# Thirty token-row dot products of a gated-expert kernel: from one VectorE reduction each to a GpSimd product and a ScalarE accumulating copy

## The reference, cut to what matters

```python
s = jnp.einsum('nhpc,hpkc->nhpk', q, sub_keys)
ts, ti = lax.top_k(s, PEER_TOPK)
...
gate = jax.nn.softmax(best_s, axis=-1)
act = jax.nn.gelu(jnp.einsum('nd,nhkd->nhk', xi, u[idx]), approximate=False)
return jnp.einsum('nhk,nhkd->nd', gate * act, v[idx])
```

## Time and profile before

| what | value |
|---|---|
| median of 3 runs | 2467.96 us (2465.28 to 2469.02) |
| the profiled execution, its own time | 2466.73 us |
| its span | 2465.0 us |
| busy share PE, DVE, ACT, POOL | 95%, 69%, 43%, 25% |
| chain that ended last, by engine | PE 74%, DVE 14%, issue 4%, POOL 3% |
| gate tiles | from 892.59 us to 1089.4 us of the span |
| granted TensorE clock in the gate tiles | 1.00 of full speed (2.4 GHz) |

### The profile page before, as it was taken

How to read it: one execution, slowest core, us unless ns; L and a number is a source line. 1 busy time by engine, 2 the same in 40 slices (tenths; PEclk the granted TensorE clock), 3 DMA queues, 4 the chain that set the end, 5 groups by cost and what they waited for, 6 DMA issues and landing times.

```text
span 2465.0 us, 38176 instructions
## 1 busy us (share of the span) xinstructions
PE 2336.5 (95%) x13568; PEld 1302.4 (53%) x13568; DVE 1707.9 (69%) x2979; ACT 1050.0 (43%) x1496; POOL 612.7 (25%) x494
## 2 busy tenths in 40 slices
PE   7998788999999998989999999988999999999998
PEld 3446664555555566655555555563454444443453
DVE  5326674568899989987888888878353438777235
ACT  4255333565666664543333333344422224333234
POOL 0003361277677651123322222204000010000001
PEclk9998999999999999999999999999999999999999
DMA  5200003378788778889999999923233323332321
GB/s 177 77 26 1 1 1 102 124 263 302 279 302 319 253 226 320 331 305 362 389 361 362 359 362 362 363 95 94 86 112 103 101 77 105 102 102 94 103 85 52
DMA packets 164871, 470.79 MB, mean 191 GB/s; under 512 B 17616, under 2 KB 70736, under 8 KB 163984
## 3 DMA queue, kind: packets, MB, share of 16 engines
q1 hardware_dynamic: 109312, 289.59, 34.3%
q0 software_dynamic: 36864, 134.23, 14.8%
q10 hardware_dynamic: 18576, 45.36, 4.9%
HBM read 421.67 MB, written 47.45 MB: 190 GB/s over the span
## 4 chain that ended last, share of the span: by engine, by line
PE 74%; DVE 14%; issue 4%; POOL 3%; ACT 2%; DMA 2%; DVEq 1%; SPq 0%; POOLq 0%; ACTq 0%
PE psum L537 23%; PE psum L538 23%; PE psum L539 23%; DVE arena L2026 3%; POOL arena L682 2%; PE psum L426 1%; DMA arena<-in_urows,arena 1%; DVE arena L2064 1%; DVE arena L511 1%; DVE arena L2061 1%; DVE arena L2065 1%; POOL arena L517 1%; DVEq L1951 1%; DVE arena L1868 0%; POOL arena L2335 0%
## 5 line engine op out<-in xcount | busy, mean ns | idle before, releaser
L537 PE MATMUL psum<-arena 128*128 128x384 f16 (+3 forms) x3648 | 1261.5, 347 | 34.2 <-DVE arena L467 13.2
L538 PE MATMUL psum<-arena 128*128 128x384 f16 (+3 forms) x3648 | 1264.6, 347 | 0.0
L539 PE MATMUL psum<-arena 128*128 128x384 f16 (+3 forms) x3648 | 1258.0, 346 | 0.0
L537 PEld LDWEIGHTS psum<-arena 128*128 128x128 f16 (+1 forms) x3648 | 354.1, 97 | 366.0 <-issue 50.5
L539 PEld LDWEIGHTS psum<-arena 128*128 128x128 f16 (+1 forms) x3648 | 353.9, 97 | 324.0 <-issue 8.1
L538 PEld LDWEIGHTS psum<-arena 128*128 128x128 f16 (+1 forms) x3648 | 353.6, 97 | 312.0 <-issue 8.4
L511 DVE SCALAR_TENSOR_TENSOR arena<-arena 128x1024 f16<-128x1024 f32 x216 | 267.4, 1240 | 307.9 <-ACT arena L498 307.4
L498 ACT ACTIVATE arena<-arena 128x1024 f16<-128x1024 f32 x216 | 226.4, 1050 | 259.5 <-PE psum L539 243.0
L1619 ACT ACTIVATE arena<-arena 128x1024 f16<-128x1024 f32 x128 | 135.3, 1057 | 298.9 <-PE psum L539 282.8
L517 POOL TENSOR_TENSOR arena<-arena 128x1024 f16<-128x1024 f32 x104 | 214.7, 2064 | 108.3 <-ACT arena L506 106.6
L2335 POOL DMA_INDIRECT arena<-in_v,arena x128 | 133.0, 1039 | 355.4 <-DVE arena L2037 323.6
(11 more groups left out here) (254 smaller groups left out, 2236.9 us busy)
## 6 DMA issues: line engine op xcount, KB each, us to landing
arena<-in_w SPq DMA_DIRECT2D x320, 512.0 KB
arena<-in_v SPq DMA_DIRECT2D x128, 512.0 KB
early_activations<-arena ACTq DMA_DIRECT2D x124, 192.0 KB
arena<-early_activations SPq DMA_DIRECT2D x124, 192.0 KB
gate_matrix<-arena ACTq DMA_DIRECT2D x5, 4096.0 KB, 16.0
arena<-gate_matrix SPq DMA_DIRECT2D x32, 640.0 KB
arena<-in_xT SPq DMA_DIRECT2D x4, 512.0 KB, 5.5
arena<-in_urows,arena POOLq DMA_INDIRECT x128
```

The lines of the kernel that those rows point to most:

```text
L537: nc.tensor.matmul(ps, a_h, b_h, start=first, stop=False)
L538: nc.tensor.matmul(ps, a_h, b_l, start=False, stop=False)
L539: return nc.tensor.matmul(ps, a_l, b_h, start=False, stop=last)
```

## The change

`TILE_DOTS` goes. The 30 dots of the gate tiles are no longer DVE instructions. ACT copies the token vectors once from PSUM into SBUF (`own_sum[0]`, free until later). POOL multiplies each fetched row with that copy, in place (`own_product`, a 128 x 1024 f32 tensor-tensor with both inputs and its output in SBUF). ACT then copies the row onto itself with a running sum (`own_total`), which gives the dot. The totals are spread evenly: number x stands behind octet floor(1.6 x) + 1. The fetch that refills a buffer waits for the total instead of the dot. The other 98 dots stay. The two renamed semaphores of another stage (`vstd_out` folded into `vsq_out`) change no order and no operation.

```diff
-TILE_DOTS = (0, 2, 4, 5, 6)
+TILE_PICKS = 5
...
@@ ScalarE
             for e in range(WOVEN + GAP, TILES_AT):
                 spilled(e)
+            act.wait_ge(own_turned, 1)
+            nc.scalar.activation(own_sum[0], own_tok, ACT.Copy).then_inc(own_acted, 1)
             cuts.cut = cut_high
+
+            def own_total(x):
+
+                act.wait_ge(own_multiplied, x + 1)
+                k = HEAD_PICKS + x
+                row = own_row(row_buffer(k))
+                nc.scalar.activation(row, row, ACT.Copy, accum_out=own_dot[:, k:k + 1]).then_inc(own_dotted, 1)
...
                     h = i + i // 4
                     if h % 2 or i % 4 == 3:
                         spilled(e + h // 2)
+                    for x in range(GT * TILE_PICKS):
+                        if x * GT * OCT // (GT * TILE_PICKS) + 1 == t * OCT + i:
+                            own_total(x)
...
@@ VectorE
-                picks = HEAD_PICKS + t * TILE_PICKS
...
-                    if i in TILE_DOTS:
-                        own_dots(picks + TILE_DOTS.index(i), 1)
...
             for e in range(TAIL_AT, NK):
                 i = e - TAIL_AT
                 cuts.upto(min(N_U + e + 3, N_POOL - 1))
+                if i == 0:
+                    dve.wait_ge(own_dotted, PICKS - TAIL_PICKS)
                 if i < 4:
                     own_dots(PICKS - TAIL_PICKS + 2 * i, 2)
                 if i == 6:
-                    dve.wait_ge(own_acted, 1)
+                    dve.wait_ge(own_acted, 2)
...
@@ GpSimd
             pool.wait_ge(head_done, PH)
+            def own_product(x):
+
+                b, use = row_use(HEAD_PICKS + x)
+                pool.wait_ge(own_in[b], use * 16 + 16)
+                nc.gpsimd.tensor_tensor(own_row(b), own_row(b), own_sum[0], ALU.mult).then_inc(own_multiplied, 1)
+
+            pool.wait_ge(own_acted, 1)
+            own_product(0)
             for k in range(HEAD_PICKS + ROWS_G, 2 * PICKS):
+                x = k - ROWS_G + 1 - HEAD_PICKS
+                if x < GT * TILE_PICKS:
+                    own_product(x)
                 own_fetch(k)
```

More of the change, by code:

```diff
@@ L95 @@
 HEAD_PICKS = (PH - 2) * TURN_PICKS
-TILE_DOTS = (0, 2, 4, 5, 6)
+TILE_PICKS = 5
 TAIL_PICKS = 8
 LEAD = GRP
-TILE_PICKS = len(TILE_DOTS)
 def row_buffer(k):
@@ L634, in build @@
         own_in = [sem(f"own_in{i}") for i in range(ROWS)]
-        own_dotted, own_added = sem("own_dotted"), sem("own_added")
+        own_multiplied, own_dotted, own_added = sem("own_multiplied"), sem("own_dotted"), sem("own_added")
         a_high = sem("a_high")
@@ L641, in build @@
         zpool_out, pool_cut, y_cut = sem("zpool_out"), sem("pool_cut"), sem("y_cut")
-        v_out, vsq_out, vstd_out, v_normed = sem("v_out"), sem("vsq_out"), sem("vstd_out"), sem("v_normed")
+        v_out, vsq_out, v_normed = sem("v_out"), sem("vsq_out"), sem("v_normed")
         u_out, mix_done, mix_read, sgu_cut = sem("u_out"), sem("mix_done"), sem("mix_read"), sem("sgu_cut")
@@ L1695, in _ @@
             nc.scalar.activation(vrs[:, 0:TT], vss[:, 0:TT], ACT.Sqrt, bias=EPSC,
-                                 scale=1.0 / D).then_inc(vstd_out, 1)
+                                 scale=1.0 / D).then_inc(vsq_out, 1)
             for n in range(N_SU, N_GA):
@@ L2192, in _ @@
             cuts.upto(N_SV + 11)
-            dve.wait_ge(vstd_out, 1)
+            dve.wait_ge(vsq_out, TT + 1)
             dchain.link(nc.vector.reciprocal(vrs[:, 4:8], vrs[:, 0:4]))
```

## The result

| | before | changed |
|---|---|---|
| median of 4 runs | 2467.8 us | 2522.2 us (2519.5 to 2527.2) |
| ratio to before, 95% interval | | 1.0224 [1.0206, 1.0243] |
| span of the profiled execution | 2465.0 us | 2521.5 us |
| POOL busy, share of the span | 25% | 29% |

The change costs 54 us; the forecast was 26 us more than before, with a range that ended at 2508. The direction is right, the size is half. The next two answer to the earlier trace rows. The periods now come in pairs of 81 us (two tiles), 40.4 us a tile on the mean instead of 31.57.

What follows compares the result with a forecast made beforehand. DVE was taken to bound the gate tiles. Dots -34.2, holds +64.8, copy +1.0 and waits -4.9 summed to +26.7 us, giving a forecast of 2494 us, range 2478 to 2508.

Steps and rivals of the forecast that it cites:

- Where the kernel is bound: Gate tiles: DVE sets the pace, busy 30.75 us of each 31.57 us period, with PE next and transfers close behind.
- The floor: Gate tiles with only the dots removed: transfers would end a tile at 28.9 us, 16 us faster at most.
- -34.2 for the dots: DVE's queue in the gate tiles: thirty dots of 1.14 us each removed, -34.2 us.
- The product's duration, 2.36: POOL's in-place f32 product over 1024 elements takes 2.36 us, between bounds of 2.00 and 2.55.
- +64.8 for the holds: Gate tiles: each POOL product delays DVE instructions with two SBUF inputs by 2.16 us; 30 products, +64.8 us.
- +1.0 for the copy: ACT's one copy of the token vectors stands ahead of a high cut that DVE waits for: +1.0 us.
- Totals free on ACT: Gate tiles: five totals, 6.3 us a tile, cost nothing as long as ACT's idle time covers them.
- -4.9 for the waits: Gate tiles: DVE's six waits of 0.82 us for ACT's high cut vanish because DVE is later, -4.9 us.
- Nobody waits for rows: Gate-tile row buffers: a row lands 8.8 us after issue, against some 14 us between fetch and product.
- The third rival: Gate tiles: ACT becomes late, one 1 us wait at each of 30 totals, +57 us in all, 2524; chance 0.06.
- two octets of lead: Gate tiles: POOL reaches a product about two octets before ACT wants its total; the argument against ACT becoming late.
- signs listed: Changed profile: tile period 35 to 36 us, 30 instructions stretched about 2.1, DVE never idle, PE waiting 25 longer, DMA 0.8.

Runs made afterwards that it cites:

- e1: Changed kernel without its 30 POOL products; ACT's totals wait for the fetched rows and sum them raw: 2450.1 us, ratio 0.9935 to the kernel before.
- e5: Kernel before with a second, idle DVE reduction at each of the 30 gate-tile dots: 2504.8 us, ratio 1.0147.
- e10: Changed kernel with ACT's totals one octet later: 2511.6 us, ratio 1.0181 to the kernel before.
- e4: Kernel before, dots kept, plus 30 idle accumulating copies on ACT at the places of the totals: 2470.0 us, ratio 1.0013.
- e9: Changed kernel without products (totals sum raw rows), plus two plain DVE reductions at five octets of a tile: 2505.4 us, ratio 1.0165 to the kernel before.
- e3: Kernel before, dots kept, plus an idle POOL product behind each of the 30 tile fetches: 2540.9 us, ratio 1.0307.
- e12: e10 with each POOL product held until an octet's first one-hot has ended: 2502.0 us, ratio 1.0142 to the kernel before.
- v2: Kernel before with dots paired on DVE and 11 of 30 low cuts moved to POOL beside them, one more ACT copy each: 2451.2 us, ratio 0.9946.

## Why the prediction was wrong

By its own steps:

- **Where the kernel is bound**: right. **The floor**: right in its number (e1 has 28.52 us a tile and 16.1 us less, against 28.9 and 16), wrong in its cause. 365 GB/s is not the most that the kernel before moves: it moves 392 in 1180:1220, and e1's tiles reach 372. What ends e1's tile is PE, 27.5 us by the prediction's own sum plus short waits for one-hots.
- **-34.2 for the dots**: right as a price; e5 puts the same amount back for 36.1.
- **The product's duration, 2.36**: right to the digit (2.36 to 2.37 wherever it is not waiting). The estimate of 2.25 from the Trainium skill's page (GPSIMD Engine Reference, section 3.1) is 0.11 low for this in-place form.
- **+64.8 for the holds**: measured 57.0, in e10 63.7. The 2.16 each is right for a product alone (2.85 less 0.68 is 2.17). Behind a fetch it is 0.4 more (3.28). And the products that run while DVE waits hold nobody: 25 of the 30 stretch a DVE instruction, 14 a one-hot and 11 a low cut. The two nearly cancel.
- **+1.0 for the copy**: not separable; the first one-hot starts 2.6 us later than before, and in other runs anywhere from 7 us earlier to 3 us later.
- **Totals free on ACT**: right for their own time (e4, e9), wrong for their place in ACT's order (below).
- **-4.9 for the waits: this step failed.** Measured +30.2. Three things stand behind it. (a) The text let the six small waits vanish because DVE would be later. Without contention that may happen (e9: of the 5.6 us, 5.02 is the first wait of all) or not (e5: 8.5 of 9.1). (b) "Nobody waits for rows", "covered": the 14 us of lead were counted with an issue of 0.94 us. The trace has 11.27, since POOL is locked out while DVE runs back to back, and the removed dots had been the openings (longest issue 1.15 us before, 1.74 in e3, 1.31 in e9, all with such work on DVE; 5.21 in e1, without). POOL also waits 14.7 us for rows, in five waits. Taking the totals off that chain (e10) saves 17 us of waits and 8 to 11 us of time, part of the gain going back into holds: shown. (c) With the products moved into the octets (e12) another 5 us of waits go, from whichever of two causes; 8 us stay and belong to products in a way that e9 does not reproduce. That remainder is open: irregular holds, residual lock-outs, or PE's clock, which is 0.93 of full speed in 895:1120 of e12 and 0.99 in e9 (e5 has 0.93 in its tiles without extra waits, but no totals either).

The third rival gave 2524 and the chip 2522. Its mechanism is right in kind (ACT's totals wait, its high cut behind them holds DVE) and wrong in form: it reckoned 30 waits of 1 us, and there are two of 3.6 us. A little over half of the extra time is DVE's waits (30.2 of 54.4 us), and of those e10 takes away 17. The nearness of the number is partly luck. It was given a chance of 0.06 because "two octets of lead" was computed from uncontended durations.

Of the signs listed, the product's duration and the undisturbed rest came; the period (40.4 instead of 35.8), 30 stretched instructions (25, by 1.2 to 2.9 us), DVE without idle time, PE's extra wait (36 instead of 25) and the transfers' share (0.7 instead of 0.8) did not, and "DVE idle while ACT waits for POOL" was named as what would prove it wrong.

## What to carry to other kernels

Work moved from DVE to POOL is paid twice where DVE's remaining instructions read two SBUF inputs: in holds, and in what POOL is late with when DVE leaves it no opening. Put a POOL instruction that reads SBUF beside DVE work with an operand in PSUM, paced by a semaphore (v2), and leave such work on DVE for that purpose. And when a chain's slack is reckoned, reckon the contended duration: an indirect transfer's issue is itself a POOL instruction that can be locked out, so nothing that an in-order engine waits for should be queued behind it with no more lead than the uncontended duration.

## What the runs showed of the hardware

- A run of back-to-back DVE instructions with two SBUF inputs can keep POOL out for its whole length, over 15 instructions: 11.27 us for the issue of an indirect transfer (0.94 alone), 10.38 for a product (2.36 alone). Each of them ends 0.8 us (the issues) or 2.2 us (the product) after DVE's last instruction. At other times POOL gets in at the next boundary: the product of 966.74 takes 2.84 us, 0.48 more than alone, until the one-hot beside it has ended. What decides between the two was not found. The Trainium skill (SBUF — State Buffer, "SBUF: two separate sides") gives the lock to whoever starts first, for one instruction; by that POOL would wait for one instruction, 1.21 us at most, and the measurement decides otherwise.
- A POOL copy with one SBUF input holds such a DVE instruction (1.2 us for 1.04), 30 memsets of 0.97 us leave the ratio at 1.0007 [0.9998, 1.0017].
- The granted TensorE clock, 1.00 (2.4 GHz) in the tiles before, is 0.83 on the mean of 991:1031 of the changed kernel. PE waits for one-hots for 7.82 us there, until 999.66; the clock is 1.00 in 991:994, 0.95 in 994:997 and 0.50 (1.2 GHz) in 997:1003. Over the tiles the 128-column matmuls take 239 ns on the mean instead of 225. In e5 they take 236, and DVE's waits did not grow there.
